# Output projection begun inside the sample fold, and three hand-overs of the memory attention moved

## The reference, cut to what matters

```python
z = rmsnorm(x) @ w_in                       # q_lat, kv_lat, k_rope, lru_x, lru_gate
attn = mla(...)                             # 8 heads; the sample reads a paged cache of 4096 rows
rec  = rg_lru(...) * gelu(lru_gate)
x = x + concat(attn, rec) @ w_out           # the output projection
x = x + mem_attend(rmsnorm(x))              # 4 heads, 256 memory rows; q, then softmax, then w_mem_o
x = x + relu(rmsnorm(x) @ w_up) ** 2 @ w_down
y = rmsnorm(x)
```

## Time and profile before

| | us |
|---|---|
| Median of 3 runs (lowest, highest) | 1043.11 (1041.83, 1044.47) |
| The profiled execution, its own time | 1043.43 |
| Its span, first to last instruction | 1041.6 |

### The profile page before, as it was taken

One profiled execution on the slowest core, in us unless ns is written; L12 is line 12 of the kernel. 1 busy time (PEld: TensorE's weight loads), 2 busy tenths in 40 slices (PEclk: granted clock), 3 DMA queues, 4 the chain that ended last, 5 costly groups with the idle time before them and its releaser, 6 DMA issues.

```text
span 1041.6 us, 19818 instructions
## 1 busy us (share of the span) xinstructions
PE 995.8 (96%) x8516; PEld 901.2 (87%) x8516; DVE 515.3 (49%) x724; ACT 298.1 (29%) x599; POOL 445.2 (43%) x282
## 2 busy tenths in 40 slices
PE   4999999889999999999998999999999999999997
PEld 4989998656777776899975699999999999999996
DVE  3889998467555555364146266431242134114413
ACT  5333365466444443121045221210120012002212
POOL 3445679501011112455320065556555555555651
PEclk9999999999899999999999999999999999999999
DMA  6422355522557773722194022332232233233222
GB/s 179 116 77 73 95 170 147 138 92 91 204 206 281 283 280 94 276 81 82 42 382 143 2 82 83 90 91 81 83 100 82 82 96 88 82 91 92 82 81 86
DMA packets 140556, 130.39 MB, mean 125 GB/s; under 512 B 13477, under 2 KB 133170, under 8 KB 136630
## 3 DMA queue, kind: packets, MB, share of 16 engines
q1 hardware_dynamic: 134888, 88.55, 28.2%
q0 software_dynamic: 2304, 37.75, 9.4%
q10 hardware_dynamic: 3278, 2.83, 0.8%
HBM read 123.53 MB, written 5.03 MB: 123 GB/s over the span
## 4 chain that ended last, share of the span: by engine, by line
PE 81%; DVE 8%; POOL 3%; ACT 2%; issue 2%; DMA 2%; SPq 1%; ACTq 0%; DVEq 0%; POOLq 0%
PE gps L558 56%; PE gps L893 5%; PE aux L907 3%; PE aux L934 2%; POOL wlo L500 2%; PE gps L1025 1%; PE aux L849 1%; PE gps L1100 1%; PE aux L913 1%; PE gps L871 1%; PE gps L682 1%; PE aux L1038 1%; PE aux L1059 1%; PE aux L924 1%; DVE lt L1691 1%
## 5 line engine op out<-in xcount | busy, mean ns | idle before, releaser
L558 PE MATMUL gps<-act_hi,whi 128*128 128x272 f32 x944 | 274.6, 291 | 5.8 <-DVE act_lo L1609 3.5
L487 POOL TENSOR_SCALAR whi<-wraw 128x1024 fp32r<-128x1024 f32 (+1 forms) x110 | 114.7, 1043 | 380.3 <-PE gps L558 318.4
L558 PE MATMUL gps<-act_lo,whi 128*128 128x272 f32 x944 | 273.9, 290 | 0.0
L558 PE MATMUL gps<-act_hi,wlo 128*128 128x272 f32 x944 | 273.7, 290 | 0.0
L490 POOL TENSOR_TENSOR wlo<-wraw,whi 128x1024 fp32r<-128x1024 f32 (+1 forms) x110 | 259.9, 2363 | 9.2
L558 PE MATMUL gps<-h_hi,wlo 128*128 128x272 f32 x640 | 185.4, 290 | 0.0
L558 PE MATMUL gps<-h_hi,whi 128*128 128x272 f32 x640 | 185.1, 289 | 0.0
L558 PE MATMUL gps<-h_lo,whi 128*128 128x272 f32 x640 | 184.7, 289 | 0.0
L558 PEld LDWEIGHTS gps<-act_hi,whi 128*128 128x128 f32 x944 | 179.0, 190 | 6.3 <-issue 4.5
L558 PEld LDWEIGHTS gps<-act_hi,wlo 128*128 128x128 f32 x944 | 178.8, 189 | 0.0
L558 PEld LDWEIGHTS gps<-act_lo,whi 128*128 128x128 f32 x944 | 178.7, 189 | 0.0
(11 more groups left out here) (355 smaller groups left out, 1483.9 us busy)
## 6 DMA issues: line engine op xcount, KB each, us to landing
wraw<-in_w_up_dram SPq DMA_DIRECT2D x32, 512.0 KB, 4.1
wraw<-in_w_down_dram SPq DMA_DIRECT2D x32, 512.0 KB, 3.7
wraw<-in_w_in_dram SPq DMA_DIRECT2D x14, 512.0 KB, 4.0
kv<-in_cache_mem_k_dram SPq DMA_DIRECT2D x7, 1024.0 KB, 7.1
kv<-in_cache_mem_v_dram SPq DMA_DIRECT2D x7, 1024.0 KB, 13.2
wraw<-in_w_mem_k_dram SPq DMA_DIRECT2D x16, 256.0 KB, 3.1
wraw<-in_w_mem_v_dram SPq DMA_DIRECT2D x16, 256.0 KB, 3.2
wraw<-in_w_out_dram SPq DMA_DIRECT2D x8, 512.0 KB, 4.0
```

Of the source, the lines that this page charges most:

```text
L487: nc.gpsimd.tensor_scalar(whi[:, slot, 0:n], wraw[:, slot, 0:n], 1.0, 1.0, ALU.mult, ALU.mult).then_inc(pool_step, 1)
L558: mm = nc.tensor.matmul(out_of(a), w_of(w, k), x_of(x, k, part), start=(k == 0 and s == 0), stop=(k == k_tiles - 1 and s == 2))
```

## The change

Three edits, and one small one. **A.** `out_part(i, a, ks)` issues the three products of each k-step in `ks` for tile 44 + i, column half a. The first two tiles of the output projection are cut into such parts, k-steps 4 to 7 first, and placed between the steps of the fold; what needs the sample columns (half 1, k-steps 0 to 3) comes after `so_lo`. The fold's transposes go to `aux[0]` and `w_uv`'s result to `aux[3]`, since `gps` is in use. Tiles 44 and 45 are done 24 products apart. **B.** `key_turn` 0 waits for `tile_free[0]`, `key_turn` 2 for `tile_free[1]`, in place of both before the first. **C.** ACT runs an Exp on one column after the square root of the second norm. **D.** The sample's context transposes and their split stand in step n = 18 of the memory attention, before the last two contexts, and each k-step of tile 60 waits for its own context (`at_lo`).

```diff
@@ -961,7 +961,27 @@
...
             mm.then_inc(fold_pe, 1)
+
+            def out_part(i, a, ks):
+
+                for k in ks:
+                    for s, (w, x) in enumerate(((0, 0), (1, 0), (0, 1))):
+                        mm = nc.tensor.matmul(gps[:, 2 * i + a, 0:HALF], weights(i, 128, w, k, 0, 128),
+                                              (act_hi, act_lo)[x][:, k, T_PARTS[a]],
+                                              start=(k == 4 and s == 0), stop=(k == 3 and s == 2))
+                return mm
+
+            pe.wait_ge(gl_lo, NW)
+            pe.wait_ge(at_lo, 4)
+            pe.wait_ge(g_td, 4 * NH)
+            pe.wait_ge(g_ta, 4 * NH)
+            pe.wait_ge(tile_free[0], T_OUT // 2)
+            pe.wait_ge(tile_free[1], T_OUT // 2)
+            pe.wait_ge(w_ready, U_OUT + 1)
+            out_part(0, 0, (4, 5))
             values(NH - 1)
+            out_part(0, 0, (6, 7))
+            out_part(0, 1, (4, 5))
             pe.wait_ge(fold_dve, 2)
...
             mm.then_inc(fold_pe, 1)
+            out_part(0, 1, (6, 7))
+            out_part(0, 0, (0, 1))
             pe.wait_ge(fold_dve, 3)
...
                 mm.then_inc(fold_pe, 1)
             for g in range(2):
+                out_part(0, 0, (g + 2,))
                 pe.wait_ge(fold_dve, g + 4)
                 for c in range(2):
-                    mm = nc.tensor.transpose(gps[:, 0, 256 * c + 128 * g:256 * c + 128 * g + 128],
+                    mm = nc.tensor.transpose(aux[:, 0, 256 * c + 128 * g:256 * c + 128 * g + 128],
                                              fin[:, g, 128 * c:128 * c + 128], ident[:, :])
             mm.then_inc(fold_pe, 1)
+            pe.wait_ge(w_ready, U_OUT + 2)
+            out_part(1, 0, (4, 5, 6, 7))
 
...
             pe.wait_ge(fold_dve, 6)
             for h in range(H):
                 for c in range(2):
                     r = 64 * (h % 2)
-                    mm = nc.tensor.matmul(aux[r:r + 64, 0, TS * (h // 2):TS * (h // 2) + TS],
+                    mm = nc.tensor.matmul(aux[r:r + 64, 3, TS * (h // 2):TS * (h // 2) + TS],
                                           wuv[:, c, 64 * h:64 * h + 64], ctxa[:, c, :, TD * h:TD * h + TD],
                                           start=(c == 0), stop=(c == 1))
             mm.then_inc(so_ps, 1)
-            pe.wait_ge(gl_lo, NW)
-            pe.wait_ge(at_lo, 4)
+            out_part(1, 1, (4, 5, 6, 7))
             pe.wait_ge(so_lo, 1)
-            pe.wait_ge(g_td, 4 * NH)
-            pe.wait_ge(g_ta, 4 * NH)
-            for i in range(8):
+            out_part(0, 1, (0, 1, 2, 3)).then_inc(tile_done, 1)
+            out_part(1, 0, (0, 1, 2, 3))
+            out_part(1, 1, (0, 1, 2, 3)).then_inc(tile_done, 1)
+            for i in range(2, 8):
                 act_tile(U_OUT + i, T_OUT + i)
             for i in range(8):
                 act_tile(U_MQ + i, T_MQ + i,
@@ -1010,9 +1035,6 @@
...
-            pe.wait_ge(tile_free[0], T_MO // 2)
-            pe.wait_ge(tile_free[1], T_MO // 2)
-
             def key_turn(n):
...
@@ -1020,6 +1042,8 @@
                     pe.wait_ge(kv_in[b], 16 if b < 7 else 32)
                 if n >= 4:
                     pe.wait_ge((ks_ea, ks_ed)[n % 2], n // 2 - 1)
+                elif n % 2 == 0:
+                    pe.wait_ge(tile_free[n // 2], T_MO // 2)
                 for dd in range(2):
...
@@ -1088,6 +1112,13 @@
...
+                if n == 4 * MH + 2:
+                    pe.wait_ge(ks_o, 1)
+                    pe.wait_ge(at_exp, A_N + 4 * MH)
+                    for dd in range(2):
+                        mm = nc.tensor.transpose(aux[:, 1, 128 * dd:128 * dd + 128], sctx[:, 128 * dd:128 * dd + 128],
+                                                 ident[:, :])
+                    mm.then_inc(ks_pT, 1)
                 m = n - 3
                 if m >= 0 and m % 4 == 3:
                     h = m // 4
...
                         mm.then_inc(at_pv, 1)
-            pe.wait_ge(ks_o, 1)
-            for dd in range(2):
-                mm = nc.tensor.transpose(aux[:, 1, 128 * dd:128 * dd + 128], sctx[:, 128 * dd:128 * dd + 128], ident[:, :])
-            mm.then_inc(ks_pT, 1)
             pe.wait_ge(ks_lo, 1)
-            pe.wait_ge(at_lo, 4 + 8)
             for i in range(8):
-                act_tile(U_MO + i, T_MO + i)
+                act_tile(U_MO + i, T_MO + i, (lambda k: pe.wait_ge(at_lo, 4 + k + 1)) if i == 0 else None)
...
@@ -1495,7 +1521,7 @@
...
-            nc.scalar.copy(act_hi[:, 0:4, TP:T], aux[:, 0, 0:4 * TS].rearrange("p (k n) -> p k n", k=4)
+            nc.scalar.copy(act_hi[:, 0:4, TP:T], aux[:, 3, 0:4 * TS].rearrange("p (k n) -> p k n", k=4)
                            ).then_inc(so_hi, 1)
@@ -1509,6 +1535,7 @@
...
             raw_norm(1, "norm_mem_g")
+            nc.scalar.activation(sst[:, 2:3], ident[:, 0:1], ACT.Exp)
             for n in range(0, BD * MH, 2):
...
+                if n == 4 * MH + 2:
+                    act.wait_ge(ks_pT, 2)
+                    nc.scalar.copy(act_hi[:, :, TP:T].rearrange("p (h e) n -> p e h n", e=2),
+                                   aux[:, 1, 0:256].rearrange("p (e h n) -> p e h n", e=2, h=MH)).then_inc(ks_hi, 1)
                 m = n - 3
...
-            act.wait_ge(ks_pT, 2)
-            nc.scalar.copy(act_hi[:, :, TP:T].rearrange("p (h e) n -> p e h n", e=2),
-                           aux[:, 1, 0:256].rearrange("p (e h n) -> p e h n", e=2, h=MH)).then_inc(ks_hi, 1)
...
-            V.tensor_copy(ctxa[:, :, :, :].rearrange("p c b q -> p (c b q)"), gps[:, 0, :]).then_inc(fold_dve, 1)
+            V.tensor_copy(ctxa[:, :, :, :].rearrange("p c b q -> p (c b q)"), aux[:, 0, :]).then_inc(fold_dve, 1)
             dve.wait_ge(so_hi, 1)
-            V.tensor_tensor(act_lo[:, 0:4, TP:T], aux[:, 0, 0:4 * TS].rearrange("p (k n) -> p k n", k=4),
+            V.tensor_tensor(act_lo[:, 0:4, TP:T], aux[:, 3, 0:4 * TS].rearrange("p (k n) -> p k n", k=4),
                             act_hi[:, 0:4, TP:T].bitcast(F32), ALU.subtract).then_inc(so_lo, 1)
...
+                if n == 4 * MH + 2:
+                    dve.wait_ge(ks_hi, 1)
+                    V.tensor_tensor(act_lo[:, :, TP:T].rearrange("p (h e) n -> p e h n", e=2),
+                                    aux[:, 1, 0:256].rearrange("p (e h n) -> p e h n", e=2, h=MH),
+                                    act_hi[:, :, TP:T].bitcast(F32).rearrange("p (h e) n -> p e h n", e=2), ALU.subtract
+                                    ).then_inc(ks_lo, 1)
                 m = n - 3
...
-            dve.wait_ge(ks_hi, 1)
-            V.tensor_tensor(act_lo[:, :, TP:T].rearrange("p (h e) n -> p e h n", e=2),
-                            aux[:, 1, 0:256].rearrange("p (e h n) -> p e h n", e=2, h=MH),
-                            act_hi[:, :, TP:T].bitcast(F32).rearrange("p (h e) n -> p e h n", e=2), ALU.subtract
-                            ).then_inc(ks_lo, 1)
             raw_norm(2, T_MO, "norm_mlp_g")
```

## The result

The changed kernel took 1037.09 us (median of 5 runs, 1035.27 to 1037.59), the one before 1041.83 in the 5 runs that stand against it (1040.78 to 1044.47); the ratio is 0.9939, 95% interval 0.9925 to 0.9953, so 6.4 us less (4.9 to 7.8). Forecast were 5.3 us. The two medians alone are only 4.7 us apart; beside the experiments the kernel before ran again, with medians of 1043.3 to 1043.5 in 9 to 21 runs, and against these the changed one is 6.2 to 6.4 us shorter. By the ratio the gain is above the forecast, but its interval includes 5.3.

A forecast was written before the change was run, and what follows sets the result against it. PE, busy 96% of the span, was taken as the bound, so time could be won only where it idles or does less. Gains of A 2.59, B 0.9, C 0.0 and D 1.8 sum to 5.3 us: 1037.8 us, range 1035.6 to 1040.8.

## What to carry to other kernels

When independent matmuls are cut into pieces and put into the gaps of a serial chain, each gap is worth its length, each pair of changes to narrow tiles and back costs some 0.3 us, and the piece that signals another engine must keep enough work behind it: count that engine's turnaround in matmuls (here 4.04 / 0.1266, some 32, of which 25 were left). Gaps can also cost behind themselves, so one trace at full clock does not show that they don't. Compare such changes between marks inside a trace: the stretches A, B and D repeated to 0.02 us, where whole executions of the kernel before scattered by 4 to 7.

## What the runs showed that I had not expected

- The clock fell behind a chain of idle pieces none of which is longer than 1.1 us, in five of six traces.
- Two executions of the same code differ by up to 3 us before the fold begins, which is as much as part A is worth. Waits for weights are one part. The clock is another: from the first L811 to the first L893 the 14 traces take 16.09 to 18.75 us, the shortest with 3.4 us at the granted 0.50, the longest with 10.2, though PE is all but always busy there. What lets the clock fall in that stretch is not shown.
- Leaving narrow fp32 matmuls for products costs PE some 0.14 on top of the longer first product.
